# A two-model fp32 kernel: the SBUF start address of the activation arena `ra` moved by 16 bytes

## The reference

```python
for i in range(DEPTH):                                  # first block
    h = h + 0.5 * swiglu(rmsnorm(h, ffn1_norm[i]), ffn1_w_gu[i], ffn1_w_down[i])
    u = rmsnorm(h, mix_norm[i])
    ... = jnp.split(u @ w_in[i], split_pts, axis=-1)    # conv, latents, gates
    merged = sigmoid(g_conv) * y_conv + sigmoid(g_mla) * y_mla
    h = h + merged @ w_o[i]
    h = h + 0.5 * swiglu(rmsnorm(h, ffn2_norm[i]), ffn2_w_gu[i], ffn2_w_down[i])
    gate = sigmoid(rmsnorm(h, ple_norm[i]) @ w_ple_gate[i])
    h = h + gate * (p[i] @ w_ple_proj[i])
h = rmsnorm(h, final_norm)
for i in range(DEPTH):                                  # second block
    a = rmsnorm(h, norm_mix_pre[i]);  u = a @ w_in[i]
    mix = concat(sparse attention, convolution, pooling) @ w_out[i]
    h = h + rmsnorm(mix, norm_mix_post[i])
    m = square(relu(rmsnorm(h, norm_mlp_pre[i]) @ w_up[i])) @ w_down[i]
    h = h + rmsnorm(m, norm_mlp_post[i])
    h = h + sigmoid(h @ ple_gate[i]) * (p[i] @ ple_proj[i])
```

## Time and profile before

| | |
|---|---|
| median of 3 runs | 1929.88 us (1928.13 to 1931.04) |
| the profiled execution's own time | 1928.13 us |
| its span, first to last instruction | 1926.3 us |
| TensorE busy, matmuls | 1879.4 us, 16,060 matmuls |
| VectorE, ScalarE, GpSimd busy | 1351.0, 997.5 and 238.0 us |
| mean granted TensorE clock | 0.992 |
| read from HBM | 326.14 MB |

### The profile page before, as it was taken

One profiled execution on the slowest core, in us unless ns is written; L12 is line 12 of the kernel. 1 busy time (PEld: TensorE's weight loads), 2 busy tenths in 40 slices (PEclk: granted clock), 3 DMA queues, 4 the chain that ended last, 5 costly groups with the idle time before them and its releaser, 6 DMA issues.

```text
span 1926.3 us, 36952 instructions
## 1 busy us (share of the span) xinstructions
PE 1879.4 (98%) x16060; PEld 1859.8 (97%) x16060; DVE 1351.0 (70%) x1608; ACT 997.5 (52%) x1233; POOL 238.0 (12%) x168
## 2 busy tenths in 40 slices
PE   8999999999999999999999999998999999799999
PEld 8999999999999999999999999998999999799998
DVE  6656877775559655787785558886856689677556
ACT  6444545564447444545564446775534476654443
POOL 3000100010002000100010001563100026710000
PEclk9999999999999999999999999999999999899999
DMA  8655455465564655544556555414565453237651
GB/s 276 212 190 190 140 178 166 134 217 197 197 202 153 220 197 193 182 133 153 170 180 205 195 197 168 135 68 132 175 197 198 160 161 111 72 110 239 199 186 56
DMA packets 246533, 329.57 MB, mean 171 GB/s; under 512 B 6246, under 2 KB 218788, under 8 KB 246372
## 3 DMA queue, kind: packets, MB, share of 16 engines
q1 hardware_dynamic: 246018, 326.79, 51.4%
q0 software_dynamic: 96, 0.26, 0.1%
q10 hardware_dynamic: 258, 0.16, 0.0%
HBM read 326.14 MB, written 1.05 MB: 170 GB/s over the span
## 4 chain that ended last, share of the span: by engine, by line
PE 79%; DVE 10%; ACT 4%; POOL 4%; issue 1%; DMA 1%; SPq 0%; POOLq 0%; DVEq 0%; ACTq 0%
PE work L2036 18%; PE work L2038 18%; PE work L2037 18%; PE acc L2036 8%; PE acc L2038 8%; PE acc L2037 8%; DVE w_lo L1321 4%; POOL fa L755 2%; ACT w_hi L808 2%; DVE ra L1334 1%; POOL fa L749 1%; DVE x_rows L1355 1%; DMA raw<-in_w_in_dram 1%; PE acc L2113 1%; DVE fa L1760 1%
## 5 line engine op out<-in xcount | busy, mean ns | idle before, releaser
L1321 DVE TENSOR_TENSOR w_lo<-raw,w_hi 128x2048 fp32r<-128x2048 f32 (+2 forms) x313 | 707.8, 2265 | 103.1 <-ACT w_hi L808 101.0
L2036 PE MATMUL work<-x_rows,w_hi 128*128 128x256 f32 x2560 | 710.4, 278 | 9.6 <-DVE w_lo L1321 6.4
L2037 PE MATMUL work<-x_rows,w_hi 128*128 128x256 f32 x2560 | 705.4, 276 | 0.0
L2038 PE MATMUL work<-x_rows,w_lo 128*128 128x256 f32 x2560 | 705.4, 276 | 0.0
L808 ACT ACTIVATE w_hi<-raw 128x2048 fp32r<-128x2048 f32 (+2 forms) x313 | 577.9, 1854 | 150.1 <-PE work L2038 67.2
L2036 PEld LDWEIGHTS work<-x_rows,w_hi 128*128 128x128 f32 x2560 | 481.3, 188 | 13.8 <-issue 8.1
L2037 PEld LDWEIGHTS work<-x_rows,w_hi 128*128 128x128 f32 x2560 | 481.4, 188 | 0.3
L2038 PEld LDWEIGHTS work<-x_rows,w_lo 128*128 128x128 f32 x2560 | 481.3, 188 | 0.0
L2036 PE MATMUL acc<-ra,w_hi 128*128 128x256 f32 x1352 | 372.3, 275 | 0.0
L2038 PE MATMUL acc<-ra,w_lo 128*128 128x256 f32 x1352 | 371.9, 275 | 0.0
L2037 PE MATMUL acc<-ra,w_hi 128*128 128x256 f32 x1352 | 371.9, 275 | 0.0
(11 more groups left out here) (302 smaller groups left out, 2332.4 us busy)
## 6 DMA issues: line engine op xcount, KB each, us to landing
raw<-in_ffn_w_gu_dram SPq DMA_DIRECT2D x88, 1024.0 KB, 5.1
raw<-in_w_in_dram SPq DMA_DIRECT2D x52, 1024.0 KB, 5.4
raw<-in_ffn_w_down_dram SPq DMA_DIRECT2D x44, 1024.0 KB, 5.0
raw<-in_w_up_dram SPq DMA_DIRECT2D x32, 1024.0 KB, 5.4
raw<-in_w_down_dram SPq DMA_DIRECT2D x32, 1024.0 KB, 4.9
raw<-in_w_mla_out_dram SPq DMA_DIRECT2D x8, 1024.0 KB, 5.4
raw<-in_w_o_dram SPq DMA_DIRECT2D x8, 1024.0 KB, 5.0
raw<-in_w_ple_gate_dram SPq DMA_DIRECT2D x8, 1024.0 KB, 5.1
```

What stands on the lines that cost most here:

```text
L1321: v.tensor_tensor(w_lo[:, s, 0:n], raw[:, r, 0:n], w_hi[:, s, 0:n].bitcast(F32), ALU.subtract).then_inc(lo_done.sem, 1)
L2036: pe.matmul(dst, ah, bh, start=start and i == 0, stop=False, skip_group_check=not group)
L2037: pe.matmul(dst, ah, bl, start=False, stop=False, skip_group_check=not group)
L2038: last = pe.matmul(dst, al, bh, start=False, stop=stop and i == len(pairs) - 1, skip_group_check=not group)
```

## The change

The arena `ra` loses its four leading elements, `fa` gets eight more at its end, and the places of `gh` and `gl` in `ra` move up by 64 elements. By the same placement `ra` begins at 157,312 + 30,848 = 188,160. Nothing else differs: instructions, their order, shapes and waits are the same.

```diff
-G_ROW, G_AT = 256, (4096, 6144)
-RA_AT = 4
+G_ROW, G_AT = 256, (4160, 6208)
...
-        fa = sb("fa", [P, 7704])
-        ra = sb("ra", [P, RA_AT + 10240], F32R)[:, RA_AT:RA_AT + 10240]
+        fa = sb("fa", [P, 7712])
+        ra = sb("ra", [P, 10240], F32R)
```

## The result

The changed kernel takes 1955.91 us (median of 4 runs, 1955.05 to 1957.7) against 1929.18 for the kernel before on the same chip: 1.0139 times as long, 95% interval 1.0127 to 1.015, or 26.7 us more. The forecast was slower, 1970, within 1955 to 1983. The direction and the cause came out; the added time was a third under the forecast (26.7 us instead of 40), and the measured time stands at the low end of the range.

What follows compares the result with a forecast made beforehand. TensorE was taken to bound the kernel. 38.4 + 3.6 - 1.0 - 1.0 = +40.0 us on the profiled 1928.1 gave 1968.1, and 1970 as median since that execution ran 1.8 us below it; range 1955 to 1983.

Steps and rivals of the forecast that it cites:

- What bounds the kernel: Whole span: TensorE, busy 1879.4 of 1926.3 us, sets the end, so added matmul time goes into the span.
- The matmuls that move `ra`: `ra` over `w_hi` and `w_lo`: 5904 matmuls go from 113.3 to 119.8 ns, adding 38.4 us.
- half a loss: Rival for `ra` sequences: they never settle but wander at 118.3 ns, 1961 us; counted within the forecast's case of 0.82.
- Distance modulo 128: TensorE operand addresses: moving less weights, modulo 128 bytes, sets the pace; 112 is fast, 16 and 0 are slow.
- The floor of 111.4 ns: Lower bound for `ra` matmuls: the weight load sets 111.4 ns from start to start, at best 11 us less.
- faster: Rival for `ra` matmuls: the new address pair runs at 111.4 ns, 11 us less, 1919 us; chance 0.06.
- The read ports: Trainium skill's rule for TensorE: two independent SBUF read ports, so address changes add 0; no effect had chance 0.09.
- The neighbours: FFN and MLP loops: 60 switches from `ra` to `x_rows` each cost 0.06 us, adding 3.6 us.
- What gives some back: TensorE: `ra` runs already slow after waits give back 1.0 us, shorter waits for `w_lo` another 1.0 us.
- the ramps: `x_rows` matmuls just behind slow `ra` sequences start at 118.3 ns: 0.06 us each, 3.6 us in all.
- the step: Each `ra` matmul over `w_hi` and `w_lo` slows by 6.5 ns, 38.4 us over 5904.
- ScalarE, VectorE, other uses of `ra`: Both engines pay nothing for the address; `ra` as weights, some 500 matmuls, counted at nothing, 3 us if wrong.

Runs made afterwards that it cites:

- the map: Separate kernel of 128x256 matmul streams, not a change to this kernel: 128 pairs of moving and weight start remainders; 17 pairs go at 113.3 ns, others 116.5 to 120.1.
- e9_all_32_on: Against the kernel before: an unused 8-element buffer moves `w_hi`, `w_lo` and every buffer behind them 32 bytes on; 1930.47 us, ratio 1.0.
- e3_shift_all: Against the changed kernel: `w_hi` and `w_lo` begin 16 bytes later, `xh` and `xl` 112 bytes earlier, `ra` stays; 1993.23 us, ratio 1.032.
- e7_at_240: Against the kernel before: the arena `ra` alone 128 bytes further; 1949.97 us, ratio 1.0098.
- e1_ra_back: Against the changed kernel: the start of `ra` alone put back to 188,144, `gh` and `gl` stay moved; 1931.15 us, ratio 0.9999 to the kernel before.
- stream kernel: Separate kernel, not the two blocks: streams of equal matmuls, each with its own weight load, one pair of start remainders per stream; the kernel before's pair ran at 113.3 ns.
- e5_at_16: Against the kernel before: `x_rows` and `ra` both moved to 16 bytes past the weights' remainder modulo 256 instead of 112; 1963.44 us, ratio 1.0175.
- e8_aligned: Against the changed kernel: `xh` and `xl` at the start of `x_rows`, `w_hi` and `w_lo` 64 bytes later; 1973.67 us, ratio 1.0223.

## Why the prediction was right, and where it wasn't

**What bounds the kernel.** Right: 34.1 us of TensorE's time gave 28.3 us of span.

**The matmuls that move `ra`.** Right in kind, too large in size: 6.5 ns were taken, 5.2 measured, 38.4 us against 30.7. The rows that I took the price from (`rot_r` over `zero_r`, `w_hi` over `x_rows`, both near 120 ns) weren't the pair of the change; the map puts that pair at 118.7. The rival "half a loss", 1961, had the better number, for another reason: it had `ra` never settle, while 89 of 90 long `ra` sequences after do settle, at 118.7.

**Distance modulo 128.** Half right, and it gave the right answer here. e9_all_32_on moves all places, keeps the distance and loses nothing, so the distance does count. But e3_shift_all keeps it over weights at an odd multiple of 16 and loses 62 us, and e7_at_240 keeps it modulo 128 only and loses 19. The argument stood on three pairs of remainders, which fit several rules. That its rule named the new pair slow is in part luck: 111 of the map's 128 pairs are slow, so nearly any move off the old place would have cost something.

**The floor of 111.4 ns.** The bound was loose. None of 128 pairs is under 113.3, and with half the weight load the best of three pairs is 113.3 again, so the length of the weight load doesn't seem to set that pace. Nothing was found that would have made room for the rival "faster".

**The read ports.** The Trainium skill, "TensorE: Matmul & The Clock Gate", Part 2, Step-by-step, has the two read ports independent. The runs here don't agree: 113.3 against 120.0 ns for one shape and one moving address with only the weights' address changed, and the order turned round by a shorter weight load, say that in this kind of matmul the two reads don't go on independently. By that rule the time would have stayed at 1930.

**The neighbours.** Right in kind: 0.04 us for each return to `x_rows` instead of 0.06, and 66 returns instead of 60: 2.6 us instead of 3.6.

**What gives some back.** Too small: 1.0 us was taken for the waits, and idle time fell by 5.8. The waits for `w_lo` shrank by 1.0 us, as taken; the rest is spread over other waits, and the largest piece, 1.6 us at the GpSimd fold, came in e1_ra_back too (1.9 us), without any slower matmul. On the profiled executions the forecast was 11.7 us too high (1968.1 against 1956.44): 6.9 from TensorE's busy time (41.0 forecast with the ramps, 34.1 measured), nearly all of it the step, and 4.8 from its idle time.

**ScalarE, VectorE, other uses of `ra`.** Right: no price to be seen. The uses of `ra` as weights are 624 matmuls by the trace, not some 500, which changes nothing. Of these, `w_hi` and `w_lo` over `ra` went from 120.5 to 118.5 ns, 0.2 us on 96 matmuls.

**Left open.** What in the hardware the two reads share; whether distance 112 holds over weights at 192 and 224 too, which no kernel tried; why distance 16 has three paces in the kernel and one in each stream kernel (113.3 over weights 0, 118.7 over 128); whether distance 192 is good over some weights in the kernel, since only weights at 192 were tried; and whether two reads of other tensors, such as `ka` over `ra`, could be placed better, which wasn't tried, as they are some 500 matmuls.

## What to carry to other kernels

In a kernel that TensorE bounds, compare the start-to-start distance of equal matmuls by moving operand before anything else: a difference of 5 ns between two buffers is worth 1.4% here, and an offset of a few elements ahead of the buffer gets it back. For matmuls of 128x256 with a full weight load a good first try is the one that held here, weights on a multiple of 32 bytes and the moving operand 112 bytes past them modulo 256. Run a loop at the kernel's own remainders and shapes: three of five places were slow in the kernel that the loop had found fast 128 bytes lower, and for the one of them that was then looped where the kernel has it, the loop too had 118.7. And measure in the whole kernel, since a pair can have more paces there than a loop shows. Any edit that changes a buffer's size ahead of such a tensor moves it: pin both starts, or check them after each edit.

## What the runs showed of the hardware that was not expected

- The same pair of addresses can run at 113.3, 116.7 or 118.8 ns per matmul for up to some 190 us, and change only behind an interruption (e5_at_16). The executions of that program differ by 15 us, against 4 for the kernel before; that the paces are why is likely, but only one execution was traced. The pair of the kernel before, 112 bytes past the weights' remainder, settled at 113.3 in every stream.
- The pattern differs 128 bytes further on: 112 over 0 has 113.3 ns, 240 over 0 has 117.1 in the streams, and so have 240 over 128 and 112 over 128 in the kernel.
- Which place is good hangs on the shape: over weights 0, moving 112 beats moving 0 with 256 columns (113.3 against 120.0 ns), ties with it with 384 (173.3 both) and loses with 512 (231.1 against 226.7, which is twice 113.3).
- Distance 192 had 113.3 ns over seven of eight weight places in the map, and 117.7 where the kernel tried it (`ra` in e8_aligned).
